# Output projection merged with the two norms, the residual, the split and the first up units, by token blocks

## What is computed

```python
h = rms_norm(x, norm_mix_pre[l])
z = h @ w_in[l]                       # then three attention mixers
mix = concat([oa, ob, oc]) @ w_out[l] # 1024 x 1024
x = x + rms_norm(mix, norm_mix_post[l])
h = rms_norm(x, norm_ffn_pre[l])
x = x + rms_norm(conv_gated_mlp(h, w_up[l], ...), norm_ffn_post[l])   # w_up: 1024 x 5632
# rms_norm(x, g) = x * rsqrt(mean(x * x) + 1e-6) * g
```

## Time and profile before

| | |
|---|---|
| median of 3 runs | 4004.22 us (4004.12 to 4004.69) |
| the profiled execution, its own time | 4003.96 us |
| its span, first to last instruction | 4002.2 us |
| mean granted TensorE clock | 0.969 |
| busy: PE, DVE, ACT, POOL | 3779.0, 1903.0, 1578.5, 1186.0 us (94%, 48%, 39%, 30%) |
| stretch of the two phases, first matmul to last, layer 0 and 1 | 195.9 and 195.8 us |

### The profile page before, as it was taken

The page is one execution under the profiler, slowest core; times in us unless marked ns, Lnnn a source line. Parts: engine busy times, 40 slices in busy tenths (PEclk is TensorE's granted clock), DMA queues, the critical chain, the costliest instruction groups (busy, mean ns, idle before and its releaser), DMA issues. The chain is left out here.

```text
span 4002.2 us, 51121 instructions
## 1 busy us (share of the span) xinstructions
PE 3779.0 (94%) x18821; PEld 3088.3 (77%) x18821; DVE 1903.0 (48%) x2890; ACT 1578.5 (39%) x2485; POOL 1186.0 (30%) x852
## 2 busy tenths in 40 slices
PE   6899999999799999999869999999988999999997
PEld 5687788778488888888657867877757888888884
DVE  5104867961734433344451257689345433344336
ACT  3323777972422112221342357689433112221223
POOL 2224433421512122121432244334224122121224
PEclk8998999999899999999989989999999999999998
DMA  5322221101311111111224123211031111111113
GB/s 177 118 74 68 67 63 31 37 22 55 109 38 39 35 42 37 37 42 31 74 84 131 60 63 80 53 31 31 26 112 51 34 42 37 37 42 31 42 31 132
DMA packets 194300, 234.43 MB, mean 59 GB/s; under 512 B 13759, under 2 KB 157669, under 8 KB 193573
## 3 DMA queue, kind: packets, MB, share of 16 engines
q1 hardware_dynamic: 194125, 232.18, 19.1%
HBM read 178.05 MB, written 58.29 MB: 59 GB/s over the span
## 5 line engine op out<-in xcount | busy, mean ns | idle before, releaser
L213 PE MATMUL ps<-hh,wh 128*128 128x512 f32 (+1 forms) x3264 | 1179.8, 361 | 116.5 <-DVE wl L506 44.1
L214 PE MATMUL ps<-hl,wh 128*128 128x512 f32 (+1 forms) x3264 | 1165.0, 357 | 0.0
L215 PE MATMUL ps<-hh,wl 128*128 128x512 f32 (+1 forms) x3264 | 1162.7, 356 | 0.0
L213 PEld LDWEIGHTS ps<-hh,wh 128*128 128x128 f32 x3264 | 623.3, 191 | 216.7 <-issue 86.1
L214 PEld LDWEIGHTS ps<-hl,wh 128*128 128x128 f32 x3264 | 623.3, 191 | 92.3 <-issue 5.8
L215 PEld LDWEIGHTS ps<-hh,wl 128*128 128x128 f32 x3264 | 622.5, 191 | 88.7
L1886 POOL TENSOR_TENSOR wl<-raw,wh 128x1024 fp32r<-128x1024 f32 x128 | 306.3, 2400 | 1278.7 <-ACT wh L1815 1278.7
L1922 DVE SCALAR_TENSOR_TENSOR cb<-ps,params,cb 128x1023 f32<-128x1023 f32 (+1 forms) x176 | 147.3, 878 | 895.9 <-ACT cb L1824 895.9
L1557 DVE TENSOR_REDUCE mx<-ps 128x1 f32<-128x512 f32 x512 | 352.5, 689 | 177.8 <-PE ps L1357 107.6
L1451 ACT ACTIVATE ph<-ps 128x512 fp32r<-128x512 f32 (+1 forms) x576 | 330.2, 573 | 183.5 <-PE ps L1325 176.8
L1824 ACT ACTIVATE cb<-ps,params 128x1280 f32<-128x1280 f32 x88 | 125.1, 1421 | 666.2 <-PE ps L215 642.2
(11 more groups left out here) (169 smaller groups left out, 5071.1 us busy)
## 6 DMA issues: line engine op xcount, KB each, us to landing
raw<-in_w_up SPq DMA_DIRECT2D x88, 512.0 KB, 3.9
heads<-stage SPq DMA_DIRECT2D x38, 640.0 KB, 3.3
raw<-in_w_down SPq DMA_DIRECT2D x44, 512.0 KB, 3.5
xo<-residual SPq DMA_DIRECT2D x32, 640.0 KB, 6.4
rq<-heads SPq DMA_DIRECT2D x56, 320.0 KB, 4.9
raw<-in_w_in SPq DMA_DIRECT2D x32, 512.0 KB, 4.5
rk<-heads SPq DMA_DIRECT2D x32, 320.0 KB, 4.3
residual<-y SPq DMA_DIRECT2D x8, 1024.0 KB, 5.0
```

What stands on the lines that cost most here:

```text
L213: pe.matmul(out, wh, xh, start=(k == 0), stop=False)
L214: pe.matmul(out, wh, xl, start=False, stop=False)
L215: last = pe.matmul(out, wl, xh, start=False, stop=(k == len(pairs) - 1))
```

## The change

The two phases become one, `project_and_normalise`, and its order is by token blocks: all eight output units for block 0, then for block 1, then for block 2, and then the up units 0 and 1 block by block. All eight output weights stay in SBUF in high and low parts (`mw_hi`, `mw_lo`). Each product of a unit and a block goes to one of four rotating PSUM banks; ACT copies it out (`evacuate`) and squares it from PSUM (`square`); DVE adds the squares into `m_acc[0]`. While PE works on the next block's units, ACT and DVE do the last block's norm, residual, second norm and split. The sums over partitions are one matmul by ones for each block and norm (`sums` into bank 6, `new_sums` into bank 7), put at fixed places between PE's products: `sums(0)` behind output unit 0 of block 1, `new_sums(0)` behind unit 3 of block 1, `sums(1)` behind unit 0 of block 2, `new_sums(1)` behind unit 5 of block 2, `sums(2)` in the middle of up unit 0 on block 0, `new_sums(2)` in the middle of up unit 0 on block 1. The second squares are now added by DVE (7 for each block) before that one matmul. The roots stay in PSUM, where DVE reads them. All residual adds and all low parts of activations are DVE's; POOL only makes the ten weights' low parts, those of the two up units (8 and 9) too. Residual chunks are loaded by block (24 DMAs, 8 for each block, in place of 8 of all tokens), into a ring and into free parts of the other block's `my`; the stores are 24 in place of 3. ACT's table set is asked for at the phase's start.

```diff
...
+    c.my = [take(f"my{i}", [P, KC, 512]) for i in range(2)]
+    c.mw_hi, c.mw_lo = list(c.wh[0:2]), list(c.wl[0:2])
+    c.mw_hi += [take(f"mw_hi{n}", [P, KC, P], F32R) for n in range(2, KC)]
+    c.mw_lo += [take(f"mw_lo{n}", [P, KC, P], F32R) for n in range(2, KC)]
+    c.mx_ring = [take(f"mx_ring{i}", [P, 512]) for i in range(5)]
+    c.m_sq = [take(f"m_sq{i}", [P, 512]) for i in range(2)]
+    c.m_acc = [take(f"m_acc{i}", [P, 512]) for i in range(2)]
...
-def output_projection(nc, c, L):
+def project_and_normalise(nc, c, L):
+    OUT_BANKS = (1, 2, 4, 5)
+    R1, R2 = 6, 7
...
+        def weight(n):
+            return (c.mw_hi[n], c.mw_lo[n]) if n < KC else (c.wh[n - KC], c.wl[n - KC])
...
+                def load_raw(n, src):
+                    sp.wait_ge(w_lo, n - 1)
+                    sp.dma_start(c.raw[n % 2][:], src).then_inc(raw_arrived[n % 2], 16)
...
+                def load_x(b, k):
+                    t0, w = BLOCKS[b]
+                    sp.dma_start(x_chunk(b, k), c.s_x[:, k, t0:t0 + w]).then_inc(x_in[b], 16)
...
+                def store(b):
+                    t0, w = BLOCKS[b]
+                    for k in range(KC):
+                        wait_added(sp, b, k)
+                        sp.dma_start(c.s_x[:, k, t0:t0 + w], y_chunk(b, k)).then_inc(stored, 16)
...
+                    load_raw(n, out_unit(c, L, n))
+                for k in range(KC):
+                    load_x(0, k)
+                for i in range(2):
+                    load_raw(KC + i, up_unit(c, L, 0, i))
+                store(0)
+                sp.wait_ge(new_added, KC - 1)
+                for k in range(4, KC):
+                    load_x(1, k)
+                for k in range(2):
+                    load_x(2, k)
+                sp.wait_ge(lo_done, KC)
+                sp.wait_ge(stored, 16 * KC)
+                for k in range(4):
+                    load_x(1, k)
+                store(1)
+                sp.wait_ge(new_added, KC - 1 + 2)
+                for k in range(2, KC):
+                    load_x(2, k)
+                for i in range(2):
+                    load_raw(KC + 2 + i, up_unit(c, L, 0, 2 + i))
+                store(2)
+                for i in range(2):
+                    sp.wait_ge(raw_arrived[i], 16 * 5)
+                sp.wait_ge(stored, 16 * 3 * KC)
...
+                def out(n, b):
+                    x = KC * b + n
+                    if b == 0:
+                        pe.wait_ge(w_lo, n + 1)
+                    if x >= 4:
+                        pe.wait_ge(evacuated, x - 3)
+                        pe.wait_ge(squared, x - 3)
+                    products(bank(c, OUT_BANKS[x % 4], BLOCKS[b][1]), n, b, range(KC)).then_inc(unit_done, 1)
+                def sums(b):
+                    w = BLOCKS[b][1]
+                    pe.wait_ge(acc_added, (KC - 1) * (b + 1))
+                    if b >= 1:
+                        pe.wait_ge(scaled, KC * b)
+                    pe.matmul(bank(c, R1, w), c.ones[:], c.m_acc[0][:, 0:w], start=True, stop=True).then_inc(summed, 1)
+                def new_sums(b):
+                    w = BLOCKS[b][1]
+                    pe.wait_ge(new_added, (KC - 1) * (b + 1))
+                    if b >= 1:
+                        pe.wait_ge(normed, KC * b)
+                    pe.matmul(bank(c, R2, w), c.ones[:], c.m_acc[1][:, 0:w], start=True, stop=True).then_inc(new_summed, 1)
+                def up(u, b, between=None):
+                    o = bank(c, 3 * u + b, BLOCKS[b][1])
+                    if b == 0:
+                        pe.wait_ge(w_lo, KC + u + 1)
+                    products(o, KC + u, b, range(4))
+                    if between:
+                        between()
+                    products(o, KC + u, b, range(4, KC)).then_inc(up_done, 1)
                 for n in range(KC):
-                    pe.wait_ge(w_lo, n + 1)
+                    out(n, 0)
+                for n in range(KC):
+                    out(n, 1)
+                    if n == 0:
+                        sums(0)
+                    if n == 3:
+                        new_sums(0)
+                for n in range(KC):
+                    out(n, 2)
+                    if n == 0:
+                        sums(1)
+                    if n == 5:
+                        new_sums(1)
+                pe.wait_ge(lo_done, KC * 1)
+                up(0, 0, lambda: sums(2))
+                up(1, 0)
+                pe.wait_ge(lo_done, KC * 2)
+                pe.wait_ge(evacuated, 3 * KC)
+                pe.wait_ge(squared, 3 * KC)
+                up(0, 1, lambda: new_sums(2))
+                up(1, 1)
+                pe.wait_ge(lo_done, KC * 3)
+                up(0, 2)
+                up(1, 2)
...
+                act.preload_act_table_set(LOG_SET)
...
+                def split(n):
+                    if n >= 2:
+                        act.wait_ge(raw_arrived[n % 2], 16 * (n // 2))
+                    if n >= KC:
+                        act.wait_ge(unit_done, 2 * KC + n - KC + 1)
+                    act.activation(weight(n)[0][:], c.raw[n % 2][:], ACT.Copy).then_inc(w_hi, 1)
...
+                for n in range(3):
+                    split(n)
+                take(0, 0)
+                split(3)
+                split(4)
+                take(1, 0)
+                split(5)
+                split(6)
+                take(2, 0)
+                split(7)
+                for n in range(3, KC):
+                    take(n, 0)
...
+                evacuate(0, 2)
+                roots(1)
+                square(0, 2)
+                take(1, 2)
+                new_squares(1, range(2))
+                take(2, 2)
+                new_squares(1, range(2, 4))
+                take(3, 2)
+                new_squares(1, range(4, 6))
+                take(4, 2)
+                split(KC)
+                new_squares(1, range(6, KC))
+                take(5, 2)
+                split(KC + 1)
+                new_roots(1)
+                take(6, 2)
+                high(1, range(3))
+                take(7, 2)
+                high(1, range(3, 6))
+                roots(2)
+                high(1, range(6, KC))
+                new_squares(2, range(KC))
+                new_roots(2)
+                high(2, range(KC))
...
+                def low_weight(n):
+                    wh, wl = weight(n)
+                    pool.wait_ge(w_hi, n + 1)
+                    pool.tensor_tensor(wl[:], c.raw[n % 2][:], wh[:].bitcast(F32), ALU.subtract).then_inc(w_lo, 1)
                 for n in range(KC):
+                    low_weight(n)
+                low_weight(KC)
+                low_weight(KC + 1)
...
+                def add_square(n, b):
+                    dve.wait_ge(squared, KC * b + n + 1)
+                    if n >= 2:
+                        dve.wait_ge(acc_added, (KC - 1) * b + n - 1)
+                    dve.tensor_tensor(acc, acc, c.m_sq[n % 2][:, 0:w], ALU.add).then_inc(acc_added, 1)
+                def add_residual(b, k):
+                    y = y_chunk(b, k)
+                    dve.wait_ge(x_in[b], 16 * KC)
+                    dve.wait_ge(scaled, KC * b + k + 1)
+                    dve.tensor_tensor(y, y, x_chunk(b, k), ALU.add).then_inc(added, 1)
+                def low(b, k):
+                    t0, w = BLOCKS[b]
+                    dve.wait_ge(hi_done, KC * b + k + 1)
+                    dve.tensor_tensor(c.hl[:, k, t0:t0 + w], y_chunk(b, k), c.hh[:, k, t0:t0 + w].bitcast(F32),
+                                      ALU.subtract).then_inc(lo_done, 1)
+                def first_norm(b, between={}):
+                    dve.wait_ge(root, b + 1)
+                    for k in range(KC):
+                        y = y_chunk(b, k)
+                        dve.scalar_tensor_tensor(out=y, in0=bank(c, R1, w), scalar=c.gain[:, G_MIX_POST + k:G_MIX_POST + k + 1],
+                                                 in1=y, op0=ALU.mult, op1=ALU.mult).then_inc(scaled, 1)
+                        if k >= 1:
+                            add_residual(b, k - 1)
+                        if k in between:
+                            add_square(between[k], b + 1)
+                    add_residual(b, KC - 1)
+                def add_new_squares(b, chunks):
+                    for k in chunks:
+                        dve.wait_ge(new_squared, KC * b + k + 1)
+                        if k >= 2:
+                            dve.wait_ge(new_added, (KC - 1) * b + k - 1)
+                        dve.tensor_tensor(acc, acc, x_chunk(b, k), ALU.add).then_inc(new_added, 1)
+                def second_norm(b, between={}):
+                    dve.wait_ge(new_root, b + 1)
+                    dve.wait_ge(stored, 16 * KC * (b + 1))
+                    for k in range(KC):
+                        y = y_chunk(b, k)
+                        dve.scalar_tensor_tensor(out=y, in0=bank(c, R2, w), scalar=c.gain[:, G_FFN_PRE + k:G_FFN_PRE + k + 1],
```

(33 more changed lines are left out.)

136 lines of the change are left out of this document (104 added, 32 removed).

## The result

The changed kernel takes 3941.52 us (median of 4 runs, 3937.97 to 3942.55); the kernel before, on the same chip, 4004.45 (4004.12 to 4006.48). The ratio is 0.984, 95% interval 0.9823 to 0.9857: 1.6% faster, where 1.8% and 3930 us were forecast. They differ, and the difference turned out to matter.

A forecast was written before the change was run, and what follows sets the result against it. PE's program plus its idle stretches bound the kernel. Useful work, start, slow start, sums, stalls and restart summed to 159.1 us a layer against 195.9, winning 73.6 in two layers: 3930 us, range 3908 to 3958.

The forecast's parts named there:

- the likeliest case: Whole kernel: the summed forecast of 3930 us holds, 3925 to 3937, chance 0.55.
- the rival of a slower DVE: From 99.3 us on, DVE's chain sets the tail with dearer scalings; 3938 to 3965 us, chance 0.24.
- the table load: Before PE's first product: ACT's table load, now ahead of the first split, delays PE's start by 1.3 us.
- restart: Behind the 7.0 us stall at `new_sums(1)`: PE restarts at lowered clock, costing 1.9 us on the chain.
- The stalls: PE's waits at `new_sums(0)`, `new_sums(1)`, `sums(2)` and `new_sums(2)`: 0.9, 7.0, 0.4 and 2.3 us.
- The two small sums: Block 2's two matmuls by ones over 256 columns: 0.5 us each, within 5.4 us for all sums.
- the disputed price of the 7.0: Before `new_sums(1)`: POOL's low parts of weights 8 and 9 slow DVE's adds; 0, 3.2 or 4.8 us, 4 taken.
- The scalings: DVE's SCALAR_TENSOR_TENSOR of 512 columns in the norms, reading PSUM and SBUF: 0.66 us taken.
- The slow start: At the phase's first products: PE starts at half clock and loses 2.1 us, as before the change.
- Two smalls: 159.1: Layer's end: after the last norm at 153.0, two products with the 256 block, 2.88 us each, end at 159.1.
- no stall in block 0: Block 0's output products: two buffers give about 8 us for two weights, against 5.44 per product, so weight loading is hidden.

The follow-up runs named there:

- e0_after_again: The changed kernel measured again with no edit, on another chip: 3943.59 us, ratio 0.9846; its profiled execution took 3944.88 us.
- e1_pool_later: Against the changed kernel, POOL's low parts of weights 8 and 9 wait until DVE's second squares of block 1 are added: 3929.66 us.
- e4_table_later: Against the changed kernel, ACT's table load stands behind the first two weight splits: 3931.47 us.
- e9_fill_at_last_sum: Against the changed kernel, eight matmuls of 512 columns with unread results are added ahead of `new_sums(2)`: 3938.52 us.
- e7_ups_last: Against the changed kernel, both sums of block 2 and all low parts come before the six up products: 3982.46 us.
- first profile: The unedited changed kernel's first profiled execution: 3937.97 us.
- e8_barrier_more: Against the changed kernel, one empty phase with its barrier is added between the merged phase and the MLP: 3943.46 us.
- e3_fill: Against the changed kernel, 24 matmuls of 512 columns with unread results are added ahead of `new_sums(1)`: 3934.41 us.
- e5_together: Against the changed kernel: POOL's weights 8 and 9 wait for DVE's adds, table load behind two splits, `new_sums(1)` behind unit 6: 3917.33 us.
- e10_together_lows: `e5_together` with five of eight activation low parts per block on POOL again and unit 7's square one step earlier: 3918.71 us.

## Why the prediction was right, and which terms were mis-sized

The time lies in the range (3908 to 3958), but 4.5 us above the likeliest case's own (3925 to 3937) and so at a time that I had given to the rival of a slower DVE. It was not that rival: the mechanism was as described, and the sum was short by 6.5 us a layer in the usual execution. So the range held the time by the room that I had left for another cause. For `e0_after_again`, layer 0, from the first product's start to the last matmul: 164.3 us measured, 157.8 forecast (159.1 less the 1.3 of the table load). The steps, in order:

| from, to | forecast | measured | what made the difference |
|---|---|---|---|
| first product, `new_sums(0)` | 69.4 | 70.95 | start at half clock longer, stall 1.61 for 0.9 |
| `new_sums(0)`, `new_sums(1)` | 48.3 | 48.86 | stall 7.80 for 7.0 |
| `new_sums(1)`, `new_sums(2)` | 25.7 | 26.94 | restart 2.65 for 1.9; stalls 0.35, 2.69 for 0.4, 2.3 |
| `new_sums(2)`, last matmul | 14.4 | 17.54 | a second half-clock restart, not counted |

- **The stalls** were forecast at 0.9, 7.0, 0.4 and 2.3 us and measured at 1.61, 7.80, 0.35 and 2.69: right in place and order, 1.9 us short in sum. The two small sums were taken at 0.5 us; the earlier trace rows has ten records, five sums, in 3.1 us, so 0.6.
- **POOL beside DVE's adds** was the disputed price of the 7.0: 0, 3.2 or 4.8 by its bounds, 4 taken. The ten adds took 10.3 us for 5.3, and taking POOL away gave 4.3 of stall back: POOL's price is 4.3. The other 0.7 are the adds, mis-sized at 0.60 us for each of 512: alone, ten took 6.0 in `e1_pool_later`. The Trainium skill, "SBUF — State Buffer", section "Who interferes with whom", gives the shared port to one engine for a whole instruction; by it the estimate was 4.8, and the trace agrees in kind: adds stood for 2.15 us, nearly the whole of POOL's 2.4, in one row and in another.
- **The scalings** from PSUM were taken at 0.66 us apart, 0.75 long: the timeline has 0.74 to 0.75, also beside POOL. So the slower DVE is not what made the difference.
- **The slow start** was carried over from before (2.1 us), where PE had been idle for 9.14 us. With the table load it stands for 10.42 us, and the start was at clock 0.50 for all of its first 6 us in `e0_after_again`; with 9.14 us again (`e4_table_later`) the same 6 us had a mean of 0.70. Of the 18 starts after 10.4 us of idle in the kept traces 16 were at 0.50 or 0.51 and two at 0.74 and 0.75; all eight after 9.14 us, the two of the kernel before among them, were at 0.66 to 0.70. So about 1 us of the table load's price comes this way, most times but not always.
- **The step that failed** is the last one: "Two smalls: 159.1" lets PE run at full clock behind `new_sums(2)`. I had counted a restart behind 7.0 us of stall, from a row with 2.88 us of idle, and none behind 2.3. In `e0_after_again` the clock was at half for 6 us behind the 2.69 us stall, and the last 15 us of work took 2.9 more. `e9_fill_at_last_sum` has the same 26.9 us ahead of that sum, changes nothing but the idle time and takes the 2.9 back in both profiled stretches: so the idle time is what brought the clock down. That the fill prevents it in every execution is not shown.
- **The rest held:** no stall in block 0, no wait for residual chunks, stores or low parts; the table load 1.3; `e7_ups_last` prices the cover at 20.6 us a layer, and the barrier, which I gave no term of its own, is worth 0.8 to 0.9.

The four differences are 1.55, 0.56, 1.24 and 3.14, 6.5 us together and 13.0 for two layers: 3930.4 + 13.0 = 3943.4, against the 3944.88 of this execution; 1.5 us lie outside the two stretches. For the first profile the differences are 1.5 and 6.4, which gives 3938.3 against its 3937.97.

**What stays open.** The same stall of 2.7 us was followed by half clock for the next 6 us in five layer stretches of six (three of the changed kernel's four, both of `e8_barrier_more`), for some 3 us in both of `e1_pool_later` (22.07 and 22.16), and by full clock in the sixth and in all four of `e3_fill` and `e4_table_later`. In the five, `new_sums(2)` came 26.9 us after `new_sums(1)`; in the others 24.3 to 26.4, so what PE did ahead of the stall differs too, and no run separates the two. So that 2.9 us can be lost twice is shown; when they are lost is not predicted by anything here. The changed kernel's own spread, 3937.97 to 3944.88, is of the size of one such restart or two.

## What to carry to other kernels

When waits of a few microseconds are cut, count what they do to the clock as well: here a layer's 12.5 us of stalls and its start cost another 8.6 us of slow matmuls (164.3 less 137.8 useful, 5.4 of sums and 12.5 idle), 2.65 and 2.9 of them behind two stalls, and matmuls without a use, put into the longest wait, gave the 2.65 back. Before a subtraction or copy moves in time, look at what DVE does there: two POOL instructions of 2.4 and 2.9 us put 4.3 us onto adds on the path, and one wait that sent the first of them some 4 us later gave it back. The largest part of what the merged phase won lay in the products that cover its last norms (20.6 us of 31.5 a layer), not in the barrier saved (0.8 to 0.9).

## What the runs showed of the hardware

- A wait of 2.7 us was followed by half clock in some executions and by full clock in others, with the same program. Behind a wait of 0.88 us (`e9_fill_at_last_sum`) the clock stayed full in both layers. Behind one of 1.81 us (`e5_together`) its mean was 0.66 over 5 us, behind one of 1.60 at the same place (`e10_together_lows`) 1.00. Behind the wait of 7.80 us the sum ran at half clock each time (2.08 us for 1.12).
- In `e0_after_again`, behind the 2.69 us stall, the clock was at 0.50 over 6.00 us and at 0.99 over the 11.58 us of matmuls behind them. In `e1_pool_later` the sum behind its 2.71 us stall still took the 0.70 us of full clock, and the clock was at 0.50 from 1029 to 1031, 2 us later.
- DVE's scaling with a source in PSUM took 0.74 to 0.75 us with POOL busy or idle; adds with both sources in SBUF took 2.15 us longer when POOL had a 1024-column subtraction.
- An empty phase with its barrier cost 0.9 us of PE's time at this seam, and nothing that the kernel's time shows.
